# Retention masks between the evacuations of v's tiles, and an output product that takes the mixed rows block by block

## The reference

```python
proj = rms_norm(h, norm1_g) @ w_in                      # q, k, v, g_ret, u_hy, gate_a, gate_b
q, k = rotary(q, pos), rotary(k, pos) * 128 ** -0.5     # 4 heads of 128
v = v.reshape(B, T, 4, 256)
# retention: o = ((q k^T) * decay mask) v, forward and backward decay of each head
o = bidir_retention(q, k, v, log_gf, log_gb)
y_a = (silu(g_ret) * head_rms_norm(o)) @ w_ret_out
y_b = hyena(u_hy) @ w_hy_out
mixed = sigmoid(gate_a) * y_a + sigmoid(gate_b) * y_b
h = h + mixed @ w_o
h = h + expert_choice_moe(rms_norm(h, norm2_g), ...)    # 16 experts, 66 tokens each
return rms_norm(h, final_norm_g)[:, 16:]
```

## Time and profile before

| | before |
|---|---|
| median of three runs | 1794.79 us (1794.64 to 1796.58) |
| profiled execution | 1796.06 us, span 1794.2 us |
| busy share PE / DVE / ACT / POOL | 84% / 73% / 57% / 18% |
| mean granted clock of TensorE | 0.937 of full speed |
| chain that ended last | DMA 37%, PE 34%, DVE 14%, ACT 7% |
| PE waits between 341 and 681 us | one, 3.2 us, in the v stage |
| PE wait ahead of the output product | 3.0 us |

### The profile page before, as it was taken

How to read it: one execution, slowest core, us unless ns; L and a number is a source line. 1 busy time by engine, 2 the same in 40 slices (tenths; PEclk the granted TensorE clock), 3 DMA queues, 4 the chain that set the end, 5 groups by cost and what they waited for, 6 DMA issues and landing times.

```text
span 1794.2 us, 43227 instructions
## 1 busy us (share of the span) xinstructions
PE 1499.7 (84%) x19619; PEld 1158.3 (65%) x19619; DVE 1305.5 (73%) x806; ACT 1024.3 (57%) x663; POOL 324.9 (18%) x180
## 2 busy tenths in 40 slices
PE   7899999999999999667887778768768876876874
PEld 5466766877888887567665646656565664665552
DVE  5746656665533336769998998888899889889974
ACT  4333432435422234468776777787677777777773
POOL 1154154324100000310740111110011011011100
PEclk9799999999999999779999999899889989989997
DMA  9202202330055521669999999999999999999993
GB/s 358 84 1 83 71 1 94 95 95 24 25 219 180 167 95 60 274 238 378 407 404 401 414 407 406 403 416 409 398 415 410 401 409 409 407 398 416 423 397 109
DMA packets 109689, 484.32 MB, mean 270 GB/s; under 512 B 6043, under 2 KB 51419, under 8 KB 92908
## 3 DMA queue, kind: packets, MB, share of 16 engines
q1 hardware_dynamic: 103728, 467.19, 66.1%
q0 software_dynamic: 5040, 14.10, 2.9%
q10 hardware_dynamic: 844, 1.89, 0.3%
HBM read 470.24 MB, written 12.91 MB: 269 GB/s over the span
## 4 chain that ended last, share of the span: by engine, by line
DMA 37%; PE 34%; DVE 14%; ACT 7%; issue 3%; POOL 3%; SPq 1%; ACTq 0%; POOLq 0%; DVEq 0%
PE ps_all L1319 24%; DMA slot<-in_w_exp_gate 17%; DMA slot<-in_w_exp_down 17%; DVE wl L1255 11%; ACT wh L775 6%; PE ps_all L1435 3%; PE ps_all L1342 2%; DMA raw<-in_w_in 2%; PE ps_all L1423 1%; PE ps_all L1478 1%; DMA xn_rows<-xb 1%; DMA h_rows<-ye,tok 1%; DVE wsp L913 1%; POOL psp L470 0%; POOL psp L468 0%
## 5 line engine op out<-in xcount | busy, mean ns | idle before, releaser
L1255 DVE SCALAR_TENSOR_TENSOR wl<-slot,wh 128x4096 f16<-128x4096 f32 x184 | 809.8, 4423 | 97.9 <-ACT wh L775 97.7
L775 ACT ACTIVATE wh<-slot 128x4096 f16<-128x4096 f32 x184 | 664.5, 3616 | 229.3 <-DMA slot<-in_w_exp_down 103.0
L1648 PE MATMUL ps_all<-xcur,wl 128*128 128x66 f16 x4096 | 424.2, 198 | 186.2 <-ACT sg L781 108.1
L1648 PEld LDWEIGHTS ps_all<-xcur,wl 128*128 128x128 f16 x4096 | 398.9, 103 | 200.4 <-ACT sg L781 106.5
L1649 PE MATMUL ps_all<-xcur,wh 128*128 128x66 f16 x4096 | 424.0, 199 | 5.2 <-issue 5.2
L1650 PE MATMUL ps_all<-xcur,wh 128*128 128x66 f16 x4096 | 423.7, 201 | 1.6 <-issue 1.6
L1649 PEld LDWEIGHTS ps_all<-xcur,wh 128*128 128x128 f16 x4096 | 399.0, 101 | 4.7 <-issue 4.5
L1650 PEld LDWEIGHTS ps_all<-xcur,wh 128*128 128x128 f16 x4096 | 399.1, 101 | 1.6 <-issue 1.6
L1319 PE MATMUL ps_all<-xnt,wsp 128*128 128x272 f16 (+1 forms) x2688 | 312.6, 279 | 6.1 <-ACT acc L601 4.3
L1319 PEld LDWEIGHTS ps_all<-xnt,wsp 128*128 128x128 f16 x2688 | 265.2, 99 | 54.5 <-issue 9.3
L1662 PE MATMUL ps_all<-wh,hidt 128*66 128x512 f16 x480 | 181.8, 379 | 21.5 <-DVE wl L1255 21.3
(11 more groups left out here) (244 smaller groups left out, 1637.0 us busy)
## 6 DMA issues: line engine op xcount, KB each, us to landing
slot<-in_w_exp_gate SPq DMA_DIRECT2D x64, 2048.0 KB, 23.9
slot<-in_w_exp_up SPq DMA_DIRECT2D x64, 2048.0 KB, 21.6
slot<-in_w_exp_down SPq DMA_DIRECT2D x64, 2048.0 KB, 22.8
raw<-in_w_in SPq DMA_DIRECT2D x32, 1024.0 KB, 6.2
raw<-in_w_ret_out SPq DMA_DIRECT2D x4, 1024.0 KB, 12.1
raw<-in_w_hy_out SPq DMA_DIRECT2D x4, 1024.0 KB, 8.4
raw<-in_w_o SPq DMA_DIRECT2D x4, 1024.0 KB, 5.1
win_t<-in_c_win SPq DMA_DIRECT2D x2, 1536.0 KB, 10.2
```

The costliest lines, as they stand in the source:

```text
L775: nc.scalar.activation(wh[c % RING][:, :], slot[(c + 2) % SLOTS][:, :], ACT.Copy, scale=W_S).then_inc(S["w_hi"], 1)
L1255: nc.vector.scalar_tensor_tensor(wl[c % RING][:, :], slot[(c + 2) % SLOTS][:, :], W_S, wh[c % RING][:, :], ALU.mult, ALU.subtract).then_in ...
L1648: nc.tensor.matmul(dst, lo, xcur[:, k, 0, :], start=k == 0 and t % TIL == 0, stop=False, skip_group_check=True)
```

## The change

Three edits; the semaphore names are rearranged as well (six that nothing used are gone, `mask_part` is new).

On DVE the three mask operations of a head no longer stand ahead of the five low halves of v, but between them: the first ahead of tile 1's, the second ahead of tile 2's, the sum ahead of tile 3's. The waits for their own ends are replaced by one wait on `mask_part` ahead of the sum. On ACT the Exp comes after the five high halves instead of before them, and `rotated_high(7)` comes after the high half of tile 1. On PE the wait for all eight mixed row blocks goes; the first output product waits for each block just ahead of the block's first term, and the first three products wait for the read-out of the PSUM quarter that they write.

```diff
@@ ACT
                 if c == 0:
                     rotated_high(6)
-                    rotated_high(7)
-                act.wait_ge(S["mask_arg"], c + 1)
-                nc.scalar.activation(mask[:, c, :], marg[0][:, :], ACT.Exp).then_inc(S["mask_ready"], 1)
                 for k in range(NT):
                     ...
+                    if c == 0 and k == 1:
+                        rotated_high(7)
+                act.wait_ge(S["mask_arg"], c + 1)
+                nc.scalar.activation(mask[:, c, :], marg[0][:, :], ACT.Exp).then_inc(S["mask_ready"], 1)
@@ DVE
                 raw_lo(C_V + 2 + hh)
-                if hh:
-                    dve.wait_ge(S["mask_ready"], hh)
-                link(nc.vector.tensor_scalar(marg[0][:, :], utab[:, :], 0.0, dec[:, 16 + hh:17 + hh], ALU.max, ALU.mult))
-                link(nc.vector.tensor_scalar(marg[1][:, :], utab[:, :], 0.0, dec[:, 12 + hh:13 + hh], ALU.min, ALU.mult))
-                nc.vector.tensor_tensor(marg[0][:, :], marg[0][:, :], marg[1][:, :], ALU.add).then_inc(S["mask_arg"], 1)
                 for k in range(NT):
+                    if k == 1:
+                        if hh:
+                            dve.wait_ge(S["mask_ready"], hh)
+                        nc.vector.tensor_scalar(marg[0][:, :], utab[:, :], 0.0, dec[:, 16 + hh:17 + hh], ALU.max, ALU.mult).then_inc(S["mask_part"], 1)
+                    if k == 2:
+                        nc.vector.tensor_scalar(marg[1][:, :], utab[:, :], 0.0, dec[:, 12 + hh:13 + hh], ALU.min, ALU.mult).then_inc(S["mask_part"], 1)
+                    if k == 3:
+                        dve.wait_ge(S["mask_part"], 2 * hh + 2)
+                        nc.vector.tensor_tensor(marg[0][:, :], marg[0][:, :], marg[1][:, :], ALU.add).then_inc(S["mask_arg"], 1)
                     ...
@@ PE
-            pe.wait_ge(S["mix_split"], KD)
-            pe.wait_ge(S["mix_hi"], KD)
+            def mixed_there(i):
+                if i % 3 == 0:
+                    pe.wait_ge(S["mix_split"], i // 3 + 1)
+                    pe.wait_ge(S["mix_hi"], i // 3 + 1)
...
-                end(project(j % 3, C_O + j // 2, j % 2, mixp))
+                if j < 3:
+                    n = AT[("YB", KD - 1)] - (AT[("YB", KD - 1)] - j) % 4
+                    pe.wait_ge(S[JOBS[n][1]], JOBS[n][2])
+                if j == 0:
+                    end(project(j % 3, C_O + j // 2, j % 2, mixp, mixed_there))
+                else:
+                    end(project(j % 3, C_O + j // 2, j % 2, mixp))
```

More of the change, by code:

```diff
@@ L184 @@
         LAST_JOB.append(AT[("WO", 2 * (_n - C_O) + 1)])
[L186 to L196, removed]
+SEMS = ("ident_in consts g2_in filt_params dft_fwd dft_inv win tables w4_in xt_saved x_again g2_row gf_row out_stored sq_dve ones_set "
+        "eps_set warm rms1_sq rms1_root rms1_inv x_raw rb_ready x_scaled x_hi x_lo_d x_lo_p border conv_w wr_ready raw_hi raw_lo tile_done "
+        "filt_arg filt_red sin_ready u_evac u_used w4_ready filt_win filt_hi filt_lo g_odd g_fold g_mid z_fold zt_hi zt_split z_skip z_mul "
+        "p_sub p_sum p_hi p_lo y_done yb_prod yb_hi dec_exp dec_ln mask_part mask_arg mask_ready rot_mul rot_ready qk_hi qk_lo v_hi v_lo "
+        "sc_ready sc_hi sc_lo sq_ready sq_both rms_root silu_ready og_ready yain_prod yain_hi yain_split gate_ready mix_a mix_b mix_sum "
+        "mix_hi mix_split h_add hh_hi hh_lo sq_part sq_sum lg_done ss_done ht_evac xr_ready rms2_root rms2_inv xn2_ready logits_in lg_sub "
+        "lg_exp lg_aff work_in idx_found cols_in x_in xe_done chain w_hi w_lo xcur_hi xcur_lo chunk_used psum_free hidt_hi hidt_lo ye_ready "
+        "rows_landed fin_sq fin_root fin_ready").split()
 def build(nc, A, out, xt_rows, xn2_rows, h_rows):
```

## The result

| | before | after |
|---|---|---|
| median (lowest to highest) | 1794.79 us (1794.64 to 1796.58), 5 runs | 1786.76 us (1783.17 to 1787.62), 5 runs |
| profiled execution | 1796.06 us, span 1794.2 | 1786.76 us, span 1784.9 |
| mean granted clock | 0.937 | 0.937 |

Run side by side, the changed kernel takes 0.9947 of the time before, with a 95% interval of 0.9936 to 0.9959: 9.5 us less, 7.4 to 11.5. The median of its own five runs, 1786.76, lies inside it. Of the 2.4 us between 1787.7 and 1785.3, 1.7 are a larger gain and 0.7 the starting point, 1795.5 in place of 1794.79.

A forecast was written before the change was run, and what follows sets the result against it. PE and the DMA engines were taken to carry most of the chain. Gains of 3.24 - 0.05 + 2.96 + 1.64 = 7.79 us, against the 1795.5 us mean, gave 1787.7 us, range 1785.8 to 1791.6.

The forecast's parts named there:

- The v stage: PE's wait before tile 4 of v goes, as mask operations move between low halves: 3.24 us gained.
- The passage to the scores: Last mask's Exp ends later, so the first masked score starts 0.45 us late; cost taken as 0.05 us.
- The output product: PE's wait for the mixed row blocks after the Hyena branch goes: 2.96 us gained, plus a clock term of 1.64.
- The waits per block: Waiting for each mixed row block inside the first output product costs 0, at most 1.8 us.
- the 7.79 of the sum: Total gain in us off the profiled execution: 3.24 - 0.05 + 2.96 + 1.64.
- The clock, the step that failed: First two output products run at full instead of half rate once the wait goes: 1.64 us, bounds 0 and 1.64.
- The range: Whole kernel: 1785.8 to 1791.6 us, the low end 1.9 us below the forecast for differences between executions.
- a gain larger than forecast: Remaining case: the expert stage happens to fall better; chance 0.03.
- the clock does not come back: Rival at the first output products: half rate stays or was absent in other executions; gain 6.15 us, 1789.3; chance 0.10.
- one wait comes back: Rival: a removed PE wait returns, likeliest at the scores' start or in the output product; 1790.9 us; chance 0.07.
- The expert weights: Rival: their load stream begins at a fixed time and sets the end, so no gain arrives; 1795.5 us; chance 0.05.
- The slower loop: Rival in the expert stage: a cycle 0.8 us longer for each of 15 experts; 1799.7 us; chance 0.03.

## Why the prediction was right in its places and short in its size

**The v stage.** 3.24 us were to go and went; no later tile waits. The mask operations cost nothing between v's low halves, and the Exp's new place kept the margins: the low half of head 1's first tile was made at 382.27 + 0.40 = 382.67, where the prediction had 383.3. The stage is 3.40 us shorter, 0.16 more than the wait: v's 480 matmuls take 53.28 us in one piece and took 10.75 and 42.70 in two.

**The passage to the scores.** Taken at 0.05 with bounds 0 and 0.45; measured 0.11 in the chain, at the edge of the 0.1 that it allowed, and 0.16 for the stage, which the kernel with the earlier Exp gives back. The reading of slack against delay was right; a place where the two are 0.03 us apart costs something.

**The output product.** The wait of 2.96 went. The waits per block cost nothing (10.96 us for 96 matmuls against the 11.02 that were reckoned from two single products, and 10.97 in the kernel that waits once), far from the upper bound of 1.8. The two products take 10.96 us at a clock of 1.00 in all nine traces of kernels with this edit. Of the 4.81 us of this stage, 2.96 are the wait and 1.68 the clock; the rest, 0.17, is that the product now begins at 677.97, 0.16 us before the Hyena branch's last matmul ends (678.13). The kernel with work in the wait has 14.04 for the stage, of which 10.90 are left in the changed kernel, so the wait with this overlap costs 3.14. In the two traces that are compared here the changed places gave 8.05 us, 0.26 from the 7.79 of the sum.

**The clock, the step that failed.** The sum took 1.64 us for the half rate behind the output product's wait, as in the one trace, and nothing for v's wait, because that trace had none there. Its bounds were 0 and 1.64, so the alternative that was weighed had the loss missing in some executions, never larger. What the runs showed in its place is a loss that differs from execution to execution behind both waits: 0 three times and 1.62 us once behind v's, 1.40, 1.68 and 2.91 behind the output product's, 2.4 us for both together by the means. Filling both waits was worth 3.6 us (2.0 to 5.2). Put into the sum: 3.40 - 0.16 + 3.14 for the two stages and the Exp without the clock is 6.4, and that with 2.4 or 3.6 for the clock is 8.8 or 10.0, against the 9.5 measured first, 8.6 in the repetition. The prediction's 7.79 had 6.15 for the first part and 1.64 for the second. So the mechanism was right, and the term was sized from a single execution. How large it truly is the runs don't settle: the predicted 7.8 lies inside the measured 7.4 to 11.5 too.

The Trainium skill ("TensorE: Matmul & The Clock Gate", "Part 1: The HAM clock gate") has it that the throttle's rhythm doesn't start with the kernel, so the point of a transition varies from run to run. The traces above agree: one gap of 3.23 us in the same place cost 1.62 us once and 0 once, and one gap of 2.96 us cost 2.91 and 1.40.

**The range.** Its lower end was worked out from how far four executions of the kernel before lay apart, 1.9 us. With 24 executions on one chip the same kernel gave 1790.28 to 1796.78, with 29 on another 1788.81 to 1799.16. The traces show where: from PE's first v matmul to the end of the second output product they differ by nothing but the waits and the half rate behind them, but the first v matmul comes at 360.7 to 364.3 us in the eleven traces without work ahead of the filters, and the rest of the kernel from the second output product on takes 1093.3 to 1098.6 us in all fourteen, whatever the version. So 1.9 us was too narrow for stages that the change doesn't touch; the 0.5 us by which the result lies outside the range is well within that. The prediction gave a gain larger than forecast a chance of 0.03, and only by the expert stage.

**The rivals.** That the clock does not come back (a gain of 6.15 us) is refuted by the window at 1.00. That one wait comes back is seen only as the 0.16 us at the scores. The expert weights do not set the end: their first repeating load is 9.66 us earlier, where PE's second output product ends 8.49 us earlier. The slower loop, which needed 0.75 us more per expert, is not there: twelve turns take 758.58 us before and 758.87 after, 0.02 us a turn.

**What stays open.** The edits alone give 2.6 and 3.7 us (the mean of two each), 6.3 together, and the change 8.6 to 9.5. Each of the four has an interval of 1.4 to 2.0 us either way. Taken from the spread of all these runs, the difference of the means is 2.9 us with an interval of 0.9 to 4.9 (an estimate), so chance is not excluded but is a poor account of it. The waits themselves add up, 3.24 + 3.13 = 6.37 in the traces, so the edits alone, with 6.3, show no gain from the clock at all, which sits badly with the 3.6 us that filling both waits was worth. A rise of the loss behind one wait when the other is gone would explain both; two traces of each are too few to see that, and no run tells it from chance.

## What to carry to other kernels

A wait of PE costs its length and then, by chance, a stretch at half rate; where a stage has a gap of about 3 us, count the second part as a range from 0 to as much as the gap itself, as these traces show it, and not as what one of them happens to show. The same holds for the stages that a change doesn't touch: here they moved by 4 and 5 us from execution to execution. Read each PE group against the same shape elsewhere in the trace: 96 matmuls at 12.64 us beside 10.96 is the clock, not the matmul. Work that is put between an engine's evacuations cost nothing here, because every low half was still made before PE asked for it, which the rows said before any run; and where a wait can't be removed, work that nobody needs can still save the time behind it. It did where it ended 0.34 to 0.86 us ahead of the work that counts, and not where it ended 1.75 us ahead.

## What the runs showed of the hardware

- A gap of 2.96 us in PE's work cost 1.4, 1.7 and 2.9 us more in three executions, at a granted clock of 0.50, the lower level of 1.2 GHz; a gap of 3.2 us (3.18 to 3.24) cost 1.62 in one of four. In the trace in which it fell, the clock was still 1.00 inside the gap (374 to 375 us above) and in the first microsecond of work behind it (376 to 377), 0.56 in the next and 0.50 from 378 on.
- Useless matmuls in the gap kept the clock at 1.00 in both kernels that had them, and a remaining gap of 0.34 or 0.41 us behind them did no harm, nor one of 0.86 us ahead of the filter products; gaps of 1.75 and 1.33 us with 1.15 us of work between brought it to 0.50.
- At half rate the float32 matmuls of 64x512 take 10.54 us for twelve, at full rate 5.38: a factor of 1.96.
- Waits on semaphores that have been reached already cost nothing in a stream of matmuls, at eight blocks in 96 matmuls: 10.96 us with them, 10.97 without.
